# A two-layer decoder trunk on one core: VectorE's order of work in the first gate pair, and the small sums for lambda moved behind the squares

## The reference

```python
for l in range(DEPTH):                                   # DEPTH = 2
    ...
    lam = (jnp.exp(jnp.sum(lambda_q1[l] * lambda_k1[l]))
           - jnp.exp(jnp.sum(lambda_q2[l] * lambda_k2[l])) + lam_init)
    ...
    h = h + _conv_glu(_rms_norm(h, ffn_norm_g[l]), w_gate_up[l], conv_w[l], conv_b[l], w_down[l])

def _conv_glu(xn, w_gate_up, conv_w, conv_b, w_down):
    g, u = jnp.split(xn @ w_gate_up, 2, axis=-1)         # 1024 -> 2 x 2816
    g = causal depthwise conv of width 3 over g, plus conv_b
    return (jax.nn.silu(g) * u) @ w_down
```

## Time and profile before

| | |
|---|---|
| median of 3 runs | 3166.21 us (3165.74 to 3167.91) |
| the profiled execution | 3166.92 us, span 3165.1 us from first to last instruction |
| TensorE busy | 3033.6 us, 96% of the span |
| VectorE busy | 2067.1 us, 65% |
| ScalarE busy | 1429.8 us, 45% |
| GpSimd busy | 746.8 us, 24% |
| granted TensorE clock, mean | 0.983 of full |

### The profile page before, as it was taken

One profiled execution on the slowest core, in us unless ns is written; L12 is line 12 of the kernel. 1 busy time (PEld: TensorE's weight loads), 2 busy tenths in 40 slices (PEclk: granted clock), 3 DMA queues, 4 the chain that ended last, 5 costly groups with the idle time before them and its releaser, 6 DMA issues.

```text
span 3165.1 us, 40336 instructions
## 1 busy us (share of the span) xinstructions
PE 3033.6 (96%) x15272; PEld 2521.0 (80%) x15272; DVE 2067.1 (65%) x3329; ACT 1429.8 (45%) x2413; POOL 746.8 (24%) x386
## 2 busy tenths in 40 slices
PE   7998999999999999999999989899999999999998
PEld 5787886788877888878877978778888788887887
DVE  6577887443469999842447788763443898997234
ACT  6358866432453333321324797653342533333112
POOL 1122026321121222232221300552202122223221
PEclk8998999999999999999999989999999999999999
DMA  6553750511112222252254467114102122224222
GB/s 206 163 160 97 156 123 10 149 47 40 31 43 80 80 80 89 85 165 72 94 139 121 132 155 152 49 36 143 47 21 57 47 90 80 80 80 144 93 75 74
DMA packets 313793, 299.99 MB, mean 95 GB/s; under 512 B 19824, under 2 KB 275312, under 8 KB 313344
## 3 DMA queue, kind: packets, MB, share of 16 engines
q1 hardware_dynamic: 305312, 280.63, 31.2%
q10 hardware_dynamic: 8288, 16.78, 1.6%
HBM read 219.71 MB, written 77.66 MB: 94 GB/s over the span
## 4 chain that ended last, share of the span: by engine, by line
PE 76%; DVE 9%; ACT 9%; issue 3%; DMA 2%; POOL 1%; SPq 0%; DVEq 0%; ACTq 0%; POOLq 0%
PE ps L2131 38%; PE ps L2396 8%; PE ps L2398 8%; PE ps L2397 8%; ACT above L1040 4%; PE ps L2166 3%; PE ps L2320 2%; PE ps L2261 2%; PE ps L2198 1%; PE ps L2313 1%; PE ps L2199 1%; PE ps L2370 1%; DVE p_a L1828 1%; ACT p_a L1195 1%; PE ps L2251 1%
## 5 line engine op out<-in xcount | busy, mean ns | idle before, releaser
L892 POOL TENSOR_TENSOR w_lo<-raw,w_hi 128x1024 fp32r<-128x1024 f32 (+4 forms) x172 | 361.5, 2107 | 1124.9 <-ACT w_hi L962 1123.3
L2131 PE MATMUL ps<-xs_hi,w_hi 128*128 128x512 f32 (+1 forms) x1728 | 540.3, 394 | 18.1 <-POOL w_lo L892 13.6
L2131 PE MATMUL ps<-xs_lo,w_hi 128*128 128x512 f32 (+1 forms) x1728 | 537.0, 392 | 0.0
L2131 PE MATMUL ps<-xs_hi,w_lo 128*128 128x512 f32 (+1 forms) x1728 | 536.1, 392 | 0.0
L1866 DVE TENSOR_TENSOR h_t<-h_t,ps 128x1024 f32<-128x1024 f32 x96 | 117.1, 1220 | 494.8 <-PE ps L2131 470.3
L2131 PEld LDWEIGHTS ps<-xs_hi,w_hi 128*128 128x128 f32 (+1 forms) x1728 | 323.5, 189 | 95.4 <-issue 19.8
L2131 PEld LDWEIGHTS ps<-xs_lo,w_hi 128*128 128x128 f32 (+1 forms) x1728 | 325.5, 188 | 71.0
L2131 PEld LDWEIGHTS ps<-xs_hi,w_lo 128*128 128x128 f32 (+1 forms) x1728 | 325.4, 188 | 71.0
L962 ACT ACTIVATE w_hi<-raw 128x1024 fp32r<-128x1024 f32 (+4 forms) x148 | 124.7, 851 | 471.6 <-PE ps L2131 411.7
L920 POOL TENSOR_SCALAR p_a<-p_a,rca 128x1024 f32<-128x1024 f32 (+7 forms) x96 | 178.4, 1869 | 422.7 <-DVE rca L1801 422.7
L2396 PE MATMUL ps<-xs_hi,w_hi 128*128 128x512 f32 x672 | 262.0, 390 | 3.7 <-DVE xs_lo L1964 3.5
(11 more groups left out here) (342 smaller groups left out, 6163.2 us busy)
## 6 DMA issues: line engine op xcount, KB each, us to landing
raw<-in_w_gu SPq DMA_DIRECT2D x48, 512.0 KB, 4.6
act_spill<-cv SPq DMA_DIRECT2D x44, 512.0 KB, 6.1
raw<-in_w_in SPq DMA_DIRECT2D x32, 512.0 KB, 5.3
qk_spill<-t_hi SPq DMA_DIRECT2D x24, 512.0 KB, 2.6
qk_spill<-t_lo SPq DMA_DIRECT2D x24, 512.0 KB, 2.8
k_b<-qk_spill SPq DMA_DIRECT2D x32, 384.0 KB
gate_e<-in_w_gu SPq DMA_DIRECT2D x20, 512.0 KB, 4.0
up_e<-in_w_gu SPq DMA_DIRECT2D x20, 512.0 KB, 5.4
```

The costliest lines, as they stand in the source:

```text
L892: nc.gpsimd.tensor_tensor(w_lo[s][:, w], raw[s][:, w], w_hi[s][:, w].bitcast(f32), ALU.subtract).then_inc(lo_done, 1)
L2131: ins = M(dst[0:c, a:b], w[s][:, k * c:(k + 1) * c], xt[:, a:b], start=(at == 0 and w is w_hi and part == 0), stop=(at == kc - 1 and w is ...
```

## The change

In pair 1 the three steps of each X7 block are moved one product later on VectorE and on ScalarE. VectorE's addition L2041 thereby stands ahead of the first X7 sum. At the start of the program the mask cast and the four dot products for lambda go behind the low parts and the squares. No operation is added or removed.

```diff
@@ ScalarE, pair f, product i
                         product_hi(q + 4)
                         if i == 0:
                             gate_silu(f - 1)
-                        if f == 1 and i < len(BLOCKS_THEN[2]):
-                            high_blocks(BLOCKS_THEN[2][i:i + 1])
+                        if f == 1 and i:
+                            high_blocks(BLOCKS_THEN[2][i - 1:i])
@@ VectorE, start of the program
             assert tw[0] == TAB_STEPS
+            dve.wait_ge(pack_dma, 16)
+            for k in range(KC):
+                gained_low(0, G_MIX, 0, k)
+            for k in range(1, KC):
+                add_square(0, k)
             dve.wait_ge(const_dma, 48)
             V.tensor_copy(cmask_r[:, :], cmask_f[:, :]).then_inc(const_done, 1)
             for l in range(DEPTH):
...
-            dve.wait_ge(pack_dma, 16)
-            for k in range(KC):
-                gained_low(0, G_MIX, 0, k)
-            for k in range(1, KC):
-                add_square(0, k)
             dve.wait_ge(lam_step, 2 * DEPTH + 1)
@@ VectorE, pair f, product i
                         product_sum(q + 5)
                         if f == 1:
-                            sum_blocks(BLOCKS_THEN[2][i:i + 1])
-                            low_blocks(BLOCKS_THEN[2][i - 1:i] if i else [])
+                            sum_blocks(BLOCKS_THEN[2][i - 1:i] if i else [])
+                            low_blocks(BLOCKS_THEN[2][i - 2:i - 1] if i > 1 else [])
```

## The result

The changed kernel takes 3168.56 us (median of 20 runs, 3164.39 to 3177.36) against 3163.49 us for the kernel before (median of 20, 3160.31 to 3170.43). The ratio is 1.0016, 95% interval 1.0010 to 1.0022: it is slower by 0.16%, some 5 us, which is more than noise and less than the 0.2% that was called a change. The 3166.21 us of the kernel before that the prediction started from was a median of three runs; with 20 it is 2.7 us lower. So the comparison to make is a predicted loss of 2.8 us with a measured one of 5.1 us (3.2 to 7.0 by the interval).

The account below looks back on a forecast made before the run. TensorE held 76% of the chain; in pair 1 `second_read`, then the making of X7 blocks, limited it. Twice 1.41 us, 2.8 us, with 0 for the start, on the 3166.21 us median gave 3169.0 us, range 3165.0 to 3171.3.

Parts of the forecast that it names:

- the order's part: Pairs 1 and 2 of both layers: the new order of work loses 1.41 us a layer, together 2.8 us.
- The first gain: Pair 1, layer 0: `kept` starts at 947.14, so product 3 starts at 947.95, 2.73 us sooner.
- What takes it back: Pair 1: product 4 keeps only 1.20 us of the gain; the last X7 low part then ends 2.01 us later.
- a ring between two engines: X7 blocks of pair 1: work alternates between ScalarE and VectorE, 3.20 us from one block's sum to the next.
- a price that decides: Pair 1: `kept` passes GpSimd's L912; the X1 low parts, reading two buffers, are held until about 949.97 instead.
- The rival that rested on their not being held: No change: GpSimd doesn't hold the X1 low parts; loss 0 to 0.1 us a layer, 3166 us, chance 10%.
- The start: Program start: low parts start some 1.2 us sooner, moved operations hide in VectorE's idle time; taken as 0.
- the term for TensorE's clock: Behind the last X7 block: one fall costs 1.5 us a layer, giving 3172.0; any fall 11%, over 6.3 us 4%.
- the prediction's own sign: Pair 1's stretch: the forecast would be wrong if TensorE's granted clock there fell below full.
- Its sign that no two X7 sums come closer than 3.2 us: Pair 1 on VectorE: the forecast would be wrong if X7 sums came closer than 3.2 us to each other.
- The rival "faster": Product 3's 2.73 us, or half, stay in both layers: 3160.8, or 3159.6 with the start; chance 8%.

Follow-up runs that it names:

- the fifth experiment: Changed kernel with pair 1's last X7 low part ahead of the two gs operations and the w_lo: 3166.90 us against 3165.04 us before, ratio 1.0009.
- the fourth experiment: Kernel before with only `kept` (L2041) of pair 1 put ahead of the first X7 sum: 3164.11 us against 3163.64 us, ratio 1.0001.
- the second experiment: Kernel before with only the move at the program's start: 3164.71 us against 3163.64 us, ratio 1.0001.
- the one with filled stops: Changed kernel plus five unused matmuls before each of pair 1's second, third and fourth X7 blocks: 3163.20 us against 3163.64 us before, ratio 1.0007.
- sixth: Kernel before with `kept` ahead of the first X7 sum and pair 1's other three X7 sums together: 3162.04 us against 3165.04 us, ratio 0.9995.
- seventh: The sixth's kernel with pair 1's two convolution taps behind `kept` of pair 2, silu one product later: 3163.65 us against 3165.04 us before, ratio 0.9994.
- the first experiment: Kernel before with only the gate pair's moves, without the move at the start: 3169.07 us against 3163.64 us, ratio 1.0018.

## Why the prediction was right, and where it was off

**The time itself: close by luck.** The measured 3168.56 us lies 0.4 us from the 3169.0 of the forecast, because a starting value that was 2.7 us too high and a loss that was 2.3 us too small nearly cancel. The scatter was taken as a microsecond from three runs; with 20 of each kernel its standard deviation is 2.8 us before and 3.5 us in the changed kernel.

**The direction, and the size of the order's part: right.** The forecast was a small loss inside 0.2%, 1.41 us a layer by the order of the work. With the clock held up, the runs show 1.28 and 1.31. (36 spacings of 0.227 us behind 967.34 end at 975.51 and not at 975.53, so the forecast's own sum is 1.39.)

**"The first gain": right.** `kept` passes GpSimd's L912, and product 3 follows 0.10 us behind its end. Counted from the start of L2031, it starts at 2.52 us (942.73 less 940.21) and before at 5.28 (950.68 less 945.40), so 2.76 us sooner; 2.73 were expected.

**"What takes it back": right step by step.** On the scale of the kernel before (5.19 us later) product 4 starts at 952.52 (expected 952.48), the X7 sums at 953.54, 956.75, 959.96 and 962.57 (expected 953.51, 956.71, 959.92 and 962.53), and TensorE reaches the last block at 966.56 (expected 966.53). Where the prediction put this down to a ring between two engines, the fifth experiment is more exact: 1.65 of the 2.04 us by which the last low part is late are the three operations that it was moved behind.

**The hold by GpSimd, "a price that decides": shown.** The X1 low parts took 4.08 us, 1.60 more than before. The rival that rested on their not being held falls by this row and by the 2.28 us of the X7 sum in the fourth experiment. The Trainium skill (SBUF — State Buffer, "Who interferes with whom") says that a `tensor_tensor` with both inputs in SBUF contends with a GpSimd instruction that reads there, and that the later of the two waits for the whole of the other; both rows agree, each with GpSimd's instruction begun first.

**The start: right as far as can be told,** 0 us, by the second experiment, whose interval goes from -2.2 to +3.2 us. That the cast would be held for 2.10 us was not foreseen.

**The step that fell short is the term for TensorE's clock.** The prediction left it out of the sum and gave any fall 11%, on the ground that one stop of 1.04 us had left the clock whole. It wrote "the new stops are 1.5 to 1.6 us each, but three come in a row". The clock fell in both layers of both profiles that have these stops, and in three of these four stretches by the end of the second, as in both layers of the fifth experiment. So the third stop wasn't needed. By the prediction's own sign ("if the granted clock of the stretch fell below full") this part was wrong. (Its sign that no two X7 sums come closer than 3.2 us contradicts its own sum, which has the fourth 2.61 us behind the third, as measured.)

The price was too low as well: 2.81 and 2.01 us a layer (changed kernel less the one with filled stops), where the prediction had taken 1.5 us from the earlier trace rows. That fall cost its layer nothing: the stretches before are 46.80 us in layer 0, with the clock whole, and 46.79 in layer 1, with the fall. It lay ahead of stops for VectorE, which took it up; here most of it lies behind the last block, where nothing does. The other experiments bear this out. A single stop of 2.2 to 3.6 us before product 3 or 4 stands in both layers of the kernel before and of the second, fourth, sixth and seventh experiments. During or shortly behind it the clock fell in six of these ten stretches, and the stretches of one kernel agree within 0.04 us whether it fell or not.

Together order and clock make 4.09 and 3.32 us in the profile, 7.4 us, where the medians say 5.1 and the interval ends at 7.0. From the start of L2031 in layer 0 to the end of the program the changed kernel's profile is 6.2 us longer (2225.9 against 2219.7 us), inside the interval: the parts outside the stretches are 1.2 us shorter in it. Over the nine profiles the part between the two stretches takes 1501.5 to 1505.1 us and the part behind the second 620.9 to 623.7, so one profile of each kernel can't place the difference. Whether the clock falls less in the average run than in the profiled ones stays open too: the time of a run doesn't say where its clock fell.

**The rival "faster": wrong for the reason given.** The 2.76 us did not outlast the X7 blocks.

## What to carry to other kernels

Take the biggest stop away only after asking which list ends the next one: moving the work that caused it to a later place on the same engine moves the stop, and a low part put behind three operations was worth 1.65 us where the exchange of two instructions was worth 0.6 the other way. Look at the operands before reordering around GpSimd: an operation that reads one operand from PSUM can be put into the time in which GpSimd works, one that reads two SBUF buffers was held there in every case seen (an X7 sum, an X1 low part, a `w_lo`), and so was the mask cast, which reads one. And count short stops in a row as a risk to TensorE's clock, and ask what stands behind them: a half-clock stretch ahead of a stop for another engine cost nothing here, one behind the last stop cost 2 to 2.8 us.

## What the runs showed of the hardware that was not expected

Stops of about 1.6 us in product 6, with three matmuls (about 1.0 us) between one and the next, halved the granted clock in all six stretches that have them unfilled: in two of them in the matmuls ahead of the second stop (in layer 0 of the first experiment it was 0.50 from 963.0 us, and that stop began at 963.05), in three by the end of the second, in one in the third. In layer 0 of the changed kernel it stayed there for about 7 us (0.81, 0.50 and 0.83 in the windows from 958, 962 and 966 us). In the kernel before, two stops of 0.95 and 1.04 us in the same place, with three matmuls between them, had left it whole. A longer single stop didn't decide it either: those of 3.4 to 3.6 us halved the clock in three stretches and left it whole in one, those of 2.2 us halved it in three and left it whole in three. Fifteen matmuls a layer whose results nobody reads, five in each stop, kept it at 1.00 and shortened the stretches by 2.8 and 2.0 us. And the first 940 us of the program, which no edit but the lambda move touches, took between 939.01 and 947.57 us from one profile to the next, so that two spans compared by themselves say nothing about a change of this size.
